# The last gate of a two-layer decoder trunk, with the operands of its matmuls exchanged

## The chip, the cores and the metric

The kernel runs on one core of one Trainium2 chip. The metric is the device time of one execution in microseconds (us). Engines: PE is TensorE, DVE is VectorE, ACT is ScalarE, POOL is GpSimd, SP issues most DMAs. Everything is float32; most matmuls run in the form fp32r, with each operand split into a high and a low part.

## The reference, cut to what matters

```python
D_MODEL, SEQ, PLE_DIM, DEPTH = 1024, 512, 256, 2
for i in range(DEPTH):
    h = h + mixer_i(rmsnorm(h, norm_mix[i]))          # two kinds of attention
    h = h + squared_relu_mlp(rmsnorm(h, norm_mlp[i]), w_ff1[i], w_ff2[i])
    gate = jax.nn.sigmoid(rmsnorm(h, norm_ple[i]) @ w_ple_gate[i])
    h = h + gate * (p[i] @ w_ple_proj[i])
return rmsnorm(h, final_norm)
```

The change is in the last pass through the two `gate` lines (i = 1) and in the final `rmsnorm`. `h` is 512 x 1024, `w_ple_gate[1]` is 1024 x 1024, `w_ple_proj[1]` 256 x 1024.

## The kernel before, in words

Activations lie with features on partitions: `h_b` is 8 slabs (KC) of 128 features x 512 tokens (T); a block of 128 tokens is one of NT = 4. Work is cut into units. A unit makes 128 output features for all tokens: its weights (128 rows x 8 row blocks x 128 columns, for the gate 8 + 2 with `w_ple_proj`) are loaded into `w_raw` by SP, split by ACT into `w_hi` and by DVE into `w_lo`, and multiplied on PE. Units alternate between two buffers and two PSUM banks (`unit_out`). For each row block `passes` issues three matmuls (hi x hi, hi x lo, lo x hi), with the weights stationary and 512 tokens moving:

```python
def passes(bank, w_k, hi, lo, start, stop):
    te.matmul(bank, w_k[0], hi, start=start, stop=False)
    te.matmul(bank, w_k[0], lo, start=False, stop=False)
    return te.matmul(bank, w_k[1], hi, start=False, stop=stop)
```

The order on every engine is written out by hand, and engines meet through semaphores. The gain of a norm is folded into the activations; the root of a norm multiplies the output of a unit (`scaled = unit_out * rstd`), so it is needed only when the first unit is evacuated. For that `statistics` sums the squares over partitions with a matmul against ones, ACT takes the root and DVE the reciprocal, all on 128 x 512.

The last gate (`gate_of(1, U_BG, 5, None)`) has units n = 0 to 6; the eighth is done in two halves of 256 tokens (`end_unit(0)`, `end_unit(1)`). For each unit DVE evacuates `unit_out` into `scaled`, ACT takes the sigmoid, DVE multiplies by the projection and adds the slab of `h_b`, ACT squares the slab (POOL adds up `sumsq`) and multiplies it with the final gain into `h_a`, PE turns that back to tokens on partitions (`turn_back`, four 128x128 transposes), and DVE copies it to `y_out` (`turned_back`). At the end, for each half: column sums of the squares with one-column matmuls (`end_sum`), root (`end_stat`), reciprocal, and each block of 128 tokens of `y_out` scaled by its root (`end_row`, two on DVE, two on ACT) and sent out by SP. ACT loads its table for the square root ahead, by a root of a spare column between the two halves.

An earlier stage already has tokens stationary (`values_unit`), with 512 weight columns moving.

Of the kernel before, what the change touches and what calls it, by code (L numbers as in the profile page):

```python
# [38 lines left out]
P = 128  # L39
# [203 lines left out]
def build(nc, x, p, rel_bias, a_w_qkv, a_w_o, b_w_qkv, b_w_o, lq1, lk1, lq2, lk2, subln, norm_mix,  # L243
          norm_mlp, w_ff1, w_ff2, norm_ple, w_gate, w_proj, final_norm, selector, out):
    ctx = ExitStack()
    with ctx:
# [64 lines left out]
        end_col = sb("end_col", [P, NT])  # L311
        end_scale = sb("end_scale", [P, NT])
# [24 lines left out]
        y_out = heads[:, KC * T:2 * KC * T].rearrange("p (a c) -> p a c", c=D)  # L337
        vectors = nc.dram_tensor("bias_vectors", (HEADS, VEC), F32, kind="Internal")
# [25 lines left out]
        def end_sums(hf):  # L364

            return (attn, unit_out[(U_END - 1) % 2])[hf][:, 0:NH]

# [8 lines left out]
        def end_turn_bank(hf):  # L376

            return wide_bank(2 + hf)[:, 0:HALF]

        def end_bank(n):  # L380

            return wide_bank(1 + n % 3)

# [215 lines left out]
        f_ready = sem("f_ready")  # L599
        ft_ps = sem("ft_ps")  # L600
        f_copied = sem("f_copied")
# [3 lines left out]
        end_ps = sem("end_ps")  # L605
# [55 lines left out]
        def _(sp):  # L661
# [141 lines left out]
            load_out(U_BO, 1, b_w_o[0])  # L803
            load_mlp(U_BF, 1)
# [8 lines left out]
        def _(pool):  # L813
# [44 lines left out]
            for norm in range(1, 7):  # L858
                for n in range(1, KC if norm < 6 else KC - 1):
                    pool.wait_ge(square_ready, (norm - 1) * (KC - 1) + n)  # L860
                    pool.wait_ge(sumsq_done, (norm - 1) * KC + n)
                    pool.tensor_tensor(sumsq[:, :], sumsq[:, :], square[n % 2][:, :],  # L862
                                       ALU.add).then_inc(sumsq_done, 1)


        @block.scalar
        def _(sc):
# [43 lines left out]
            def statistics(norm):  # L911
                sc.wait_ge(stat_ps, norm + 1)
                sc.activation(root[:, :], attn[:, :], ACT.Sqrt, scale=1.0 / D,
                              bias=eps_col[:, 0:1]).then_inc(root_ready, 1)
# [146 lines left out]
            def gate_of(layer, first, norm, dst):  # L1061
                for n in range(KC):
                    u = At(first + n)
                    if n == 0:
                        next_hi(u)
                        sc.wait_ge(sumsq_done, norm * KC)
                        sc.activation(sumsq_parts[:, 0, :], sumsq[:, :], ACT.Copy).then_inc(sumsq_hi_ready, 1)
# [8 lines left out]
                    slab((norm + 1) * KC + n, n, h_b, dst, gated_ready, layer * KC + n + 1)  # L1076
                    if layer == 0 and n == 1:
                        split_ple_hi(1)
                    if layer == 1:

                        col = gain_col((norm + 1) * KC + n)
                        sc.activation(h_a[:, n, :], h_b[:, n, :], ACT.Copy, scale=gains[:, col:col + 1]
                                      ).then_inc(f_ready, 1)
# [54 lines left out]
            last, w = KC - 1, 7 * KC - 1  # L1138
            gain = gains[:, gain_col(w):gain_col(w) + 1]
# [6 lines left out]
            def end_slab(hf):  # L1146
                cols = slice(hf * HALF, (hf + 1) * HALF)
                sc.wait_ge(gated_ready, 2 * KC + hf)
                sc.activation(square[w % 2][:, cols], h_b[:, last, cols], ACT.Square
                              ).then_inc(square_ready, 1)  # L1150
                sc.activation(h_a[:, last, cols], h_b[:, last, cols], ACT.Copy, scale=gain
                              ).then_inc(f_ready, 1)

            def end_stat(hf):
                sc.wait_ge(end_ps, hf + 1)
                sc.activation(end_col[:, hf * NH:(hf + 1) * NH], end_sums(hf), ACT.Sqrt, scale=1.0 / D,
                              bias=eps_col[:, 0:1]).then_inc(end_root, 1)

            def end_row(hf):
                a = hf * NH + 1  # L1160
                sc.wait_ge(f_copied, KC + hf)
                sc.wait_ge(end_rstd, hf + 1)
                sc.activation(y_out[:, a, :], y_out[:, a, :], ACT.Copy, scale=end_scale[:, a:a + 1]
                              ).then_inc(y_ready_odd, 1)

            end_sigmoid(0)
            sc.wait_ge(sumsq_done, w - 1 - KC)
            end_slab(0)
            end_sigmoid(1)

            sc.activation(spare[:, :], eps_col[:, 0:1], ACT.Sqrt)
            end_stat(0)
            end_slab(1)
            end_row(0)
            end_stat(1)
            end_row(1)
# [3 lines left out]
        def _(ve):  # L1180
# [24 lines left out]
            def statistics(norm):  # L1205
                ve.wait_ge(root_ready, norm + 1)
                ve.reciprocal(rstd[:, :], root[:, :]).then_inc(rstd_ready, 1)
# [249 lines left out]
            def turned_back(n):  # L1457

                ve.wait_ge(ft_ps, n + 1)
                ve.tensor_copy(y_out[:, :, n * P:(n + 1) * P],  # L1460
                               end_bank(n).rearrange("p (a c) -> p a c", c=P)).then_inc(f_copied, 1)

            def gate_of(layer, first, norm, dst):

                for n in range(KC):
                    u = At(first + n)
                    if n == 0:
                        next_lo(u)
                        ve.wait_ge(sumsq_hi_ready, layer + 1)
# [7 lines left out]
                    ve.tensor_tensor(scaled[:, :], unit_out[u.const % 2][:, :], rstd[:, :], ALU.mult  # L1477
                                     ).then_inc(evac_done, 1)
# [11 lines left out]
                    else:  # L1490
                        ve.tensor_tensor(h_b[:, n, :], hidden[:, :], h_b[:, n, :], ALU.add
# [5 lines left out]
                    if layer == 1 and n > 1:  # L1497
                        turned_back(n - 2)
# [102 lines left out]
            def end_evac(hf):  # L1601
                cols = slice(hf * HALF, (hf + 1) * HALF)
                ve.wait_ge(units_done, U_END + hf)
                ve.tensor_tensor(scaled[:, cols], end_unit_bank(hf), rstd[:, cols], ALU.mult
                                 ).then_inc(evac_done, 1)

            def end_gated(hf):
# [3 lines left out]
                                 ).then_inc(ple_ps_done, 1)  # L1611
                ve.wait_ge(ple_ps_done, 2 * KC + hf)
                ve.tensor_tensor(h_b[:, last, cols], hidden[:, cols], h_b[:, last, cols], ALU.add
                                 ).then_inc(gated_ready, 1)

            def end_turned(hf):
                ve.wait_ge(ft_ps, KC + hf)
                ve.tensor_copy(y_out[:, hf * NH:(hf + 1) * NH, last * P:(last + 1) * P],
                               end_turn_bank(hf).rearrange("p (a c) -> p a c", c=P)
                               ).then_inc(f_copied, 1)  # L1620

            def end_row(hf):
                a = hf * NH
                ve.wait_ge(end_root, hf + 1)
                ve.reciprocal(end_scale[:, a:a + NH], end_col[:, a:a + NH]).then_inc(end_rstd, 1)
                ve.wait_ge(f_copied, KC + hf)
                ve.wait_ge(end_rstd, hf + 1)
                ve.tensor_scalar(y_out[:, a, :], y_out[:, a, :], end_scale[:, a:a + 1], None, ALU.mult
                                 ).then_inc(y_ready_even, 1)

            turned_back(last - 2)
# [6 lines left out]
            end_row(0)  # L1638
            end_turned(1)
            end_row(1)  # L1640


        @block.tensor
        def _(te):
# [290 lines left out]
            def gate_of(layer, first, norm):  # L1935
                for n in range(KC):
                    u = At(first + n)
                    if layer == 1 and n == KC - 1:
                        break
# [17 lines left out]
                    if layer == 0 and n == 1:  # L1957
                        turn_ple(1)
                    if layer == 1 and n > 1:
                        turn_back(n - 2)  # L1960

            def turn_back(n):

                te.wait_ge(f_ready, n + 1)
                wait(te, f_copied, n - 2)
# [144 lines left out]
```

## Time and profile before

| | |
|---|---|
| median of 3 runs | 1614.56 us (1613.98 to 1615.56) |
| the profiled execution | 1614.48 us |
| its span, first to last instruction | 1612.6 us |
| PE busy | 1598.4 us |
| DVE, ACT, POOL busy | 906.3, 607.3, 65.9 us |
| mean granted clock of TensorE | 0.998 of full speed |

The span is the time between the first and the last instruction; the execution's own time is 1.9 us longer. Durations of matmuls overlap, as they are pipelined: the distance between the starts of two of them is what PE gives to one.

### The profile page before, as it was taken

The numbers are of one execution on the slowest core, as the hardware profiler recorded it, in microseconds if no ns is written. First come the engines' busy times: TensorE is split into PE (matmuls) and PEld (weight loads), VectorE is DVE, ScalarE is ACT, GpSimd is POOL, SyncE is SP. The second block draws the span as 40 slices with busy tenths as digits, with TensorE's granted clock in tenths as the row PEclk, the third lists the DMA queues.
The fourth block names the chain that finished last, engine by engine and source line by source line (L and its number), as shares of the span: only waits on it lengthen the run. The fifth ranks groups of instructions, "written<-read, shape, count | busy, mean of one in ns | idle before, by whom it ended". The sixth has DMA issues, their size and how long they took to land.

```text
span 1612.6 us, 22051 instructions
## 1 busy us (share of the span) xinstructions
PE 1598.4 (99%) x8244; PEld 1319.4 (82%) x8244; DVE 906.3 (56%) x1585; ACT 607.3 (38%) x1092; POOL 65.9 (4%) x68
## 2 busy tenths in 40 slices
PE   9999999999999999999999999999999999999998
PEld 7888888888888788888888878888878888888887
DVE  5365464464455863635455676777675363535555
ACT  5234334333333531312223445676652222222344
POOL 1000000000000200000001110000020000000111
PEclk9999999999999999999999999999999999999999
DMA  6633433433322333333333333323233333333331
GB/s 165 161 105 96 127 104 93 120 112 86 101 84 69 105 91 103 93 96 94 97 92 103 98 111 92 92 80 93 62 92 103 93 91 104 91 104 91 92 111 72
DMA packets 300571, 160.12 MB, mean 99 GB/s; under 512 B 31545, under 2 KB 295282, under 8 KB 300514
## 3 DMA queue, kind: packets, MB, share of 16 engines
q1 hardware_dynamic: 300112, 158.61, 34.6%
q0 software_dynamic: 144, 0.71, 0.2%
q8 instruction: 37, 0.61, 0.2%
q14 instruction: 20, 0.16, 0.0%
q10 hardware_dynamic: 258, 0.04, 0.0%
HBM read 157.11 MB, written 10.60 MB: 104 GB/s over the span
## 4 chain that ended last, share of the span: by engine, by line
PE 95%; POOL 1%; DVE 1%; DMA 1%; ACT 1%; issue 0%; SPq 0%; POOLq 0%; ACTq 0%; DVEq 0%
PE unit_out L1647 26%; PE unit_out L1649 26%; PE unit_out L1648 25%; PE turned L1723 2%; PE attn L1792 2%; POOL sumsq L862 1%; PE attn L2037 1%; PE unit_out L1811 1%; PE logits L1723 1%; PE unit_out L1812 1%; PE unit_out L1813 1%; DMA w_raw<-in_a_w_qkv_dram 1%; PE logits L1647 1%; PE misc L1723 1%; PE misc L1647 1%; PE misc L1649 1%
## 5 line engine op out<-in xcount | busy, mean ns | idle before, releaser
L1647 PE MATMUL unit_out<-act_hi,w_hi 128*128 128x512 f32 x1849 | 726.5, 393 | 1.4 <-DVE act_lo L1202 1.0
L1649 PE MATMUL unit_out<-act_hi,w_lo 128*128 128x512 f32 x1849 | 718.7, 389 | 0.0
L1648 PE MATMUL unit_out<-act_lo,w_hi 128*128 128x512 f32 x1849 | 718.0, 388 | 0.0
L880 ACT ACTIVATE w_hi<-w_raw 128x1024 fp32r<-128x1024 f32 (+3 forms) x256 | 271.0, 1058 | 459.4 <-PE unit_out L1649 348.2
L1647 PEld LDWEIGHTS unit_out<-act_hi,w_hi 128*128 128x128 f32 x1849 | 347.2, 188 | 76.3 <-DVE w_lo L1187 2.8
L1649 PEld LDWEIGHTS unit_out<-act_hi,w_lo 128*128 128x128 f32 x1849 | 347.1, 188 | 72.5
L1648 PEld LDWEIGHTS unit_out<-act_lo,w_hi 128*128 128x128 f32 x1849 | 347.5, 188 | 69.7 <-issue 0.2
L1187 DVE TENSOR_TENSOR w_lo<-w_raw,w_hi 128x1024 fp32r<-128x1024 f32 (+3 forms) x256 | 320.2, 1251 | 119.3 <-ACT w_hi L880 119.3
L1049 ACT ACTIVATE act_hi<-hidden 128x512 fp32r<-128x512 f32 x64 | 40.5, 633 | 243.4 <-DVE hidden L1445 243.4
L862 POOL TENSOR_TENSOR sumsq<-sumsq,square 128x512 f32<-128x512 f32 x41 | 57.8, 1410 | 1523.9 <-ACT square L908 1522.2
L1442 DVE TENSOR_TENSOR scaled<-unit_out,rstd 128x512 f32<-128x512 f32 x62 | 42.8, 690 | 67.8 <-PE unit_out L1649 67.7
L1266 DVE TENSOR_TENSOR h_a<-h_a,unit_out 128x512 f32<-128x512 f32 x39 | 26.8, 687 | 90.0 <-PE unit_out L1649 90.0
L1266 DVE TENSOR_TENSOR heads<-heads,unit_out 128x512 f32<-128x512 f32 x40 | 27.5, 686 | 84.2 <-PE unit_out L1649 84.2
L988 ACT ACTIVATE probs<-probs,w_raw 128x256 f32<-128x256 f32 (+1 forms) x128 | 61.7, 483 | 32.4 <-DVE w_raw L1290 32.4
L1448 DVE TENSOR_TENSOR act_lo<-hidden,act_hi 128x512 fp32r<-128x512 f32 x64 | 44.3, 692 | 44.7 <-ACT act_hi L1049 44.7
L1445 DVE SCALAR_TENSOR_TENSOR hidden<-scaled 128x512 f32<-128x512 f32 x64 | 44.3, 692 | 2.2
L1526 DVE CUSTOM_DVE_ANT_0 probs<-logits,bias 128x512 f32<-128x512 f32 (+3 forms) x64 | 28.2, 486 | 26.0 <-PE logits L1649 26.0
L1105 ACT ACTIVATE probs<-probs,low 128x512 f32<-128x512 f32 (+3 forms) x64 | 35.4, 554 | 7.4 <-DVE low L1526 7.4
L895 ACT ACTIVATE act_hi<-heads,gains 128x512 fp32r<-128x512 f32 x24 | 17.3, 722 | 49.1 <-DVE heads L1266 25.6
L1358 DVE TENSOR_TENSOR act_lo<-attn,act_hi 128x512 f32 (+1 forms) x8 | 5.5, 690 | 53.6 <-ACT act_hi L1002 53.6
L1275 DVE TENSOR_SCALAR probs<-probs,w_raw 128x256 f32<-128x256 f32 (+1 forms) x128 | 35.2, 339 | 0.3
L1290 DVE CUSTOM_DVE_ANT_0 probs<-logits,bias 128x256 f32<-128x256 f32 (+1 forms) x64 | 21.1, 386 | 20.4 <-PE logits L1774 20.4
(291 smaller groups left out, 1414.4 us busy)
## 6 DMA issues: line engine op xcount, KB each, us to landing
w_raw<-in_w_ff_dram SPq DMA_DIRECT2D x128, 512.0 KB, 4.0
w_raw<-in_a_w_qkv_dram SPq DMA_DIRECT2D x56, 512.0 KB, 3.9
w_raw<-in_b_w_qkv_dram SPq DMA_DIRECT2D x24, 512.0 KB, 5.1
w_raw<-in_a_w_qkv_dram SPq DMA_DIRECT2D x32, 256.0 KB, 3.0
w_raw<-in_w_ple_gate_dram SPq DMA_DIRECT2D x16, 512.0 KB, 4.1
bias_tiles_b<-bias_vectors SPq DMA_DIRECT2D x16, 256.0 KB, 4.3
bias<-bias_tiles_b SPq DMA_DIRECT2D x8, 512.0 KB, 3.7
w_raw<-in_a_w_o_dram SPq DMA_DIRECT2D x8, 448.0 KB, 3.6
```

The source lines that it names most:

```text
L862: pool.tensor_tensor(sumsq[:, :], sumsq[:, :], square[n % 2][:, :], ALU.add).then_inc(sumsq_done, 1)
L880: sc.activation(weights_of(u)[0][:, 0:width, :], w_raw[par][:, 0:width, :], ACT.Copy).then_inc(hi_done, 1)
L988: e = sc.activation(probs[i][:, cols], probs[i][:, cols], ACT.Exp, bias=low_col, scale=-1.0, accum_out=sum_col)
L1187: ve.tensor_tensor(lo[:, 0:width, :], w_raw[par][:, 0:width, :], hi[:, 0:width, :], ALU.subtract).then_inc(lo_done, 1)
L1266: ve.tensor_tensor(h[:, n, :], h[:, n, :], unit_out[u.const % 2][:, :], ALU.add).then_inc(evac_done, 1)
L1442: ve.tensor_tensor(scaled[:, :], bank_of(u)[:, :], rstd[:, :], ALU.mult).then_inc(evac_done, 1)
L1445: ve.scalar_tensor_tensor(hidden[:, :], scaled[:, :], 0.0, scaled[:, :], ALU.max, ALU.mult).then_inc(hid_ready, 1)
L1448: ve.tensor_tensor(MID[layer][1][:, n, :], hidden[:, :], MID[layer][0][:, n, :], ALU.subtract).then_inc(hid_done, 1)
L1647: te.matmul(bank, w_k[0], hi, start=start, stop=False)
L1648: te.matmul(bank, w_k[0], lo, start=False, stop=False)
L1649: return te.matmul(bank, w_k[1], hi, start=False, stop=stop)
L1723: last = te.transpose(bank[:, dst:dst + P], src, ident[:, :])
```

## The change: what it does

- In the last gate the operands of the matmuls are exchanged: a block of 128 tokens is stationary, the 128 weight columns of the unit move (`token_passes`, for each of 4 token blocks). The output has tokens on partitions and goes into the same bank, 4 blocks of 128 x 128.
- The root of the norm ahead of it has one value for each partition and block: the sum of squares comes from four one-column matmuls (`token_statistics`), root and reciprocal are on 128 x 4 instead of 128 x 512. The split of `sumsq` into high and low parts is dropped for this layer.
- The residual `h_b` is turned (`turn_h(n)`, behind unit n) instead of the sum; the eighth slab is turned ahead of the two halves.
- The final sum of squares runs along the free axis: ACT squares four blocks of 128 x 128 for each slab with an accumulator into `end_squares`, and for each half DVE adds the 8 numbers of each token (`reduce_sum`).
- The final gain, now along the free axis, is loaded as 128 copies of 1024 numbers into `end_gain` (512 KB, on SP's queue between the output projection's loads and the last MLP's), and POOL multiplies slabs 0 to 6 with it, DVE the last.
- At the end ACT has the order sigmoid 0, squares 0, sigmoid 1, root 0, squares 1, root 1, without the root of the spare column; DVE scales rows 0 to 2, ACT row 3.

```diff
@@ sync
             load_out(U_BO, 1, b_w_o[0])
+            sp.wait_ge(logits_done, ITEMS_A + B_HEADS * B_ITEMS)
+            sp.dma_start(end_gain, final_norm.rearrange("(n c) -> n c", n=1)[0:1, :].partition_broadcast(P)
+                         ).then_inc(end_gain_ready, 16)
             load_mlp(U_BF, 1)
@@ gpsimd
+            pool.wait_ge(end_gain_ready, 16)
+            for n in range(KC - 1):
+                pool.wait_ge(end_squared, n + 1)
+                pool.tensor_tensor(slab_of_y(n), slab_of_y(n), gain_of_slab(n, NT), ALU.mult
+                                   ).then_inc(y_gained, 1)
@@ scalar, gate_of
+                        sc.wait_ge(gated_ready, KC + n + 1)
+                        wait(sc, end_squared, n - 1)
+                        for a in range(NT):
+                            done = sc.activation(square[n % 2][:, a * P:(a + 1) * P],
+                                                 y_out[:, a, n * P:(n + 1) * P], ACT.Square,
+                                                 accum_out=end_squares[:, a, n:n + 1])
+                        done.then_inc(end_squared, 1)
-                        sc.activation(h_a[:, n, :], h_b[:, n, :], ACT.Copy, scale=gains[:, col:col + 1]
-                                      ).then_inc(f_ready, 1)
@@ vector, gate_of
-                        ve.tensor_tensor(h_b[:, n, :], hidden[:, :], h_b[:, n, :], ALU.add
+                        ve.wait_ge(h_turned_ps, n + 1)
+                        ve.tensor_tensor(slab_of_y(n), by_token(hidden[:, :]), by_token(end_bank(n)), ALU.add
                                          ).then_inc(gated_ready, 1)
-                    if layer == 1 and n > 1:
-                        turned_back(n - 2)
@@ vector, end
             end_evac(0)
             end_gated(0)
+            end_sum(0)
             end_evac(1)
-            turned_back(last - 1)
             end_gated(1)
-            end_turned(0)
-            end_row(0)
-            end_turned(1)
-            end_row(1)
+            end_scales(0)
+            end_row(0, y_ready_even)
+            end_row(1, y_ready_odd)
+            end_sum(1)
+            end_scales(1)
+            end_row(2, y_ready_even)
@@ tensor
+            def token_passes(bank, blocks, w_k, src, k, start, stop):
+                for n, a in enumerate(blocks):
+                    to = bank[:, n * P:(n + 1) * P]
+                    hi, lo = (x[:, k, a * P:(a + 1) * P] for x in src)
+                    te.matmul(to, hi, w_k[0], start=start and n == 0, stop=False)
+                    te.matmul(to, hi, w_k[1], start=False, stop=False)
+                    last = te.matmul(to, lo, w_k[0], start=False, stop=stop and n == len(blocks) - 1)
+                return last
+            def token_gate(first, norm):
+                ple = ple_hi[1], ple_lo[1]
+                for n in range(KC - 1):
+                    u = At(first + n)
+                    te.wait_ge(lo_done, u.const + 1)
+                    te.wait_ge(evac_done, u.const - 1)
+                    for k in range(KC):
+                        if n == 0:
+                            te.wait_ge(act_ready, norm * KC + k + 1)
+                        if n == 1 and k == 3:
+                            token_statistics(norm)
+                        token_passes(unit_out[u.const % 2], range(NT), weights(u.const % 2, k), IN[1], k,
+                                     k == 0, k == KC - 1)
...
+                    turn_h(n)
@@ tensor, end
-            turn_back(last - 2)
+            turn_h(KC - 1)
             end_unit(0)
             end_unit(1)
-            turn_back(last - 1)
-            end_sum(0)
-            end_turn(0)
-            end_sum(1)
-            end_turn(1)
```

## Rows read from the trace of the kernel before

**Rows 1.** The page: busy time by engine, and the chain by engine.
```profile
PE 1598.4 (99%) x8244; PEld 1319.4 (82%) x8244; DVE 906.3 (56%) x1585; ACT 607.3 (38%) x1092; POOL 65.9 (4%) x68
...
PE 95%; POOL 1%; DVE 1%; DMA 1%; ACT 1%; issue 0%; SPq 0%; POOLq 0%; ACTq 0%; DVEq 0%
```

**Rows 2.** Busy time in the last gate: length, each engine (instructions), clock, DMA.
```profile
1543.00:1602.00 59.00, 58.77 (x300) 49.70 (x299) 34.67 (x42) 26.25 (x36) 9.11 (x7) 1.00 0.23 67
```

**Rows 3.** Timeline of DVE (start, length): the evacuations at the gate's ends.
```profile
1543.45 0.69 DVE L1266 TENSOR_TENSOR heads<-heads,unit_out 128x512 f32<-128x512 f32 x1 [0.70 <-PE unit_out L1649]
...
1601.98 0.42 DVE L1604 TENSOR_TENSOR scaled<-unit_out,rstd 128x256 f32<-128x256 f32 x1 [1.81 <-PE misc L1649]
```

**Rows 4.** Timeline of PE and its weight loads (PEld): 512 columns, then 256.
```profile
1592.13 0.19 PEld L1647 LDWEIGHTS misc<-ple_hi,w_hi 128*128 128x128 f32 x1
...
1593.27 0.19 PEld L1649 LDWEIGHTS misc<-ple_hi,w_lo 128*128 128x128 f32 x1
...
1594.51 0.36 PE L1647 MATMUL unit_out<-act_hi,w_hi 128*128 128x256 f32 x1
...
1601.66 0.28 PE L1649 MATMUL misc<-ple_hi,w_lo 128*128 128x256 f32 x1
```

**Rows 5.** Timeline: transposes, then two fp32r loads; groups: one transpose's mean.
```profile
1593.72 1.03 PE L1723 MATMUL turned<-ident,h_a 128*128 128x128 f32 x8
...
1594.48 0.19 PEld L1647 LDWEIGHTS unit_out<-act_hi,w_hi 128*128 128x128 f32 x1
...
1594.59 0.19 PEld L1648 LDWEIGHTS unit_out<-act_lo,w_hi 128*128 128x128 f32 x1
...
L1723 PE MATMUL turned<-ident,h_a 128*128 128x128 f32 x20 | 3.1, 275 | 0.0
```

**Rows 6.** Other 128-column matmuls: timeline, then the chain, then a load group.
```profile
1059.74 0.19 PEld L1648 LDWEIGHTS logits<-qk_lo_b,qk_hi 64*128 64x128 f32 x2
...
1059.85 0.20 PEld L1649 LDWEIGHTS logits<-qk_hi,qk_lo_b 64*128 64x128 f32 x2
...
1058.31 1.05 PE L2037 MATMUL attn<-heads,probs_t 128*128 128x128 f32 x8
...
1059.29 0.39 PE L1647 MATMUL logits<-qk_hi 64*128 64x256 f32 x2
...
534.21 3.43 PE attn L1792 x60
...
L1792 PEld LDWEIGHTS attn<-probs,heads 128*64 128x64 f32 x480 | 26.0, 137 | 2.8 <-issue 2.8
```

**Rows 7.** The chain: a one-column fp32 matmul, two records.
```profile
1605.33 0.22 PE unit_out L2074 x2
```

**Rows 8.** Groups of weight loads where tokens are stationary: the second of a pair.
```profile
L1812 PEld LDWEIGHTS unit_out<-w_lo,act_hi 128*128 128x128 f32 x64 | 12.0, 188 | 2.2
```

**Rows 9.** One tile: ACT's squares with an accumulator (min/median/max ns).
```profile
L1119 ACT ACTIVATE square<-square x4: 294/295/312, 1168.0 to 1168.9; 128x128 f32<-128x128 f32 x4
```

**Rows 10.** Timeline of the tail, ACT and DVE.
```profile
1602.88 1.28 ACT L1171 ACT_TABLE_LOAD   x1
...
1604.83 0.75 DVE L1628 TENSOR_SCALAR heads<-heads,end_scale 128x1024 f32<-128x1024 f32 x1
...
1606.90 1.15 ACT L1163 ACTIVATE heads<-heads,end_scale 128x1024 f32<-128x1024 f32 x1 [0.49 <-DVE end_scale L1625]
```

**Rows 11.** SP's timeline, the chain, and the page's DMA issues (KB, us).
```profile
1174.17 0.34 SPq L675 DMA_DIRECT2D w_raw<-in_b_w_o_dram  x1
...
1178.13 3.99 DMA w_raw<-in_w_ff_dram
...
bias<-bias_tiles_b SPq DMA_DIRECT2D x8, 512.0 KB, 3.7
```

**Rows 12.** Timeline of PE at the start: transposes of the identity.
```profile
1.74 3.67 PE L1729 MATMUL unit_out<-ident 128*128 128x128 f32 x16 [1.74 <-POOL ident L819]
...
8.28 1.97 PE L1729 MATMUL unit_out<-ident 128*128 128x128 f32 x16
```

More of the change, by code:

```diff
@@ L912, in statistics @@
                 sc.wait_ge(stat_ps, norm + 1)
-                sc.activation(root[:, :], attn[:, :], ACT.Sqrt, scale=1.0 / D,
+                to, sums = (start_col[:, :], attn[:, 0:NT]) if norm == 5 else (root[:, :], attn[:, :])
+                sc.activation(to, sums, ACT.Sqrt, scale=1.0 / D,
                               bias=eps_col[:, 0:1]).then_inc(root_ready, 1)
@@ L1137, in _ @@
             gate_of(1, U_BG, 5, None)
-            last, w = KC - 1, 7 * KC - 1
-            gain = gains[:, gain_col(w):gain_col(w) + 1]
+            last = KC - 1
             def end_sigmoid(hf):
@@ L1956, in gate_of @@
                     last.then_inc(units_done, 1)
-                    if layer == 0 and n == 1:
+                    if n == 1:
                         turn_ple(1)
[L1959 to L1965, printed above, removed]
-                turn(end_bank(n), [(a * P, h_a[:, n, a * P:(a + 1) * P])
-                                   for a in range(NT)]).then_inc(ft_ps, 1)
+            def token_passes(bank, blocks, w_k, src, k, start, stop):
[6 more added lines that the diff above has]
+                return last
@@ new lines, in token_statistics @@
+            def token_statistics(norm):
+                te.wait_ge(sumsq_done, norm * KC)
+                for a in range(NT):
+                    last = te.matmul(attn[:, a:a + 1], sumsq[:, a * P:(a + 1) * P], ones[:, 0:1],
+                                     start=True, stop=True)
+                last.then_inc(stat_ps, 1)
+            def token_gate(first, norm):
[5 more added lines that the diff above has]
+                    for k in range(KC):
+                        if n == 0:
+                            te.wait_ge(act_ready, norm * KC + k + 1)
[3 more added lines that the diff above has]
+                                     k == 0, k == KC - 1)
+                    if n == 0:
+                        te.wait_ge(ple_ready, 2)
+                    te.wait_ge(ple_ps_done, KC + n - 1)
+                    for k in range(KP):
+                        last = token_passes(ple_bank(n), range(NT), weights(u.const % 2, KC + k), ple, k,
+                                            k == 0, k == KP - 1)
+                    last.then_inc(units_done, 1)
+                    turn_h(n)
@@ L1969, in _, with turn_h @@
+            def turn_h(n):
+                wait(te, gated_ready, KC + n - 2)
+                turn(end_bank(n), [(a * P, h_b[:, n, a * P:(a + 1) * P]) for a in range(NT)]
+                     ).then_inc(h_turned_ps, 1)
             out_late(0, U_AO)
@@ L2044, in _ @@
             mlp_of(1, U_BF, 4)
-            gate_of(1, U_BG, 5)
-            last, u = KC - 1, U_END - 1
+            token_gate(U_BG, 5)
+            u = U_END - 1
             def end_unit(hf):
-                cols = slice(hf * HALF, (hf + 1) * HALF)
+                blocks = range(hf * NH, (hf + 1) * NH)
                 te.wait_ge(lo_done, u + 1)
```

145 lines of the change are left out of this document (71 added, 74 removed).

## The prediction

> **What bounds the kernel now.** I read the page first, then the last 70 us stage by stage. The page gives TensorE (PE) 1598.4 us of a 1612.6 us span, and PE holds 95% of the chain that ended last [rows 1]. So a change in PE's own work is paid in full, and work on the other engines is free until it makes PE wait. The stretch that the diff rewrites is the last gate. Over 59 us of it PE is busy for 58.77, VectorE (DVE) for 34.67, ScalarE (ACT) for 26.25 and GpSimd (POOL) for 9.11 [rows 2]. PE binds here too, and the others have 40% or more of their time to spare. I measure the stage between two evacuations by DVE that wait for PE: that of the last MLP unit at 1543.45 and that of the second half of the last gate unit at 1601.98, so 58.5 us [rows 3].
>
> The question is then what one matmul costs PE, which is the distance between starts, not the duration printed beside it. In a run of 128x512 matmuls the weight loads start at 1592.13 and, five later, at 1593.27: 0.228 us each. The 60 matmuls of 128x256 in the two half units start from 1594.51 to 1601.66: 59 steps of 0.121 us [rows 4]. The stage adds up: 7 units x 30 x 0.228 = 47.9, the two statistics matmuls 0.46, six slabs of four transposes 2.6, 60 x 0.121 = 7.3, in all 58.3 of 58.5.
>
> **Where the change puts its cost: the gate's matmuls.** Before, the stationary operand is a 128x128 block of weights and the moving one 512 tokens: three matmuls for each of 8+2 row blocks of the weights, 30 a unit. After, the stationary operand is a block of 128 tokens and the moving one the 128 weight columns. That is three matmuls for each of 4 token blocks: 12 for each row block, 120 a unit. Seven units give 840, and the two halves with 2 token blocks each 2 x 60 = 120, so 960 instead of 270. The columns streamed are the same, but each matmul brings its own weight load, and there are 3.6 times as many.
>
> So the price of a 128-column matmul with a 128-column load decides everything. No row has it with all 128 rows in fp32r; the nearest are these.
> - The eight transposes with 128 columns and 128x128 loads take 1.03 us, the last of them 0.275 in its own: (1.03 - 0.275) / 7 = 0.108 each. Right after them two fp32r loads with the full 128 rows start 0.11 apart (1594.48 and 1594.59) [rows 5].
> - The score matmuls of 128 columns in fp32r, on 64 rows, go as pairs in two halves of the array. Their loads start 0.11 apart from pair to pair (1059.74, 1059.85), so a half of the array takes a load each 0.11. Eight records of an fp32 128x128 product hold PE from 1058.31 to 1059.29: 0.1225 each, at most [rows 6].
> - A matmul that streams one column and still loads 128 takes two records in 0.22 us: 0.11 each, although there is nothing to stream [rows 7].
> The last row shows that it is the load that takes 0.11, and that 128 columns of streaming (a quarter of 0.228, 0.057) vanish beneath it. I take 0.110, between 0.107 (the two 128-column spacings, rounded down) and 0.1225. Sum: 960 x 0.110 = 105.6; bounds 102.7 and 117.6.
>
> The Trainium skill, "TensorE: Matmul & The Clock Gate", section "Back-to-back issue gap", puts a stream of load and matmul pairs at about 81 ns for 128 columns, and its section on the weight path's fast load says that full loads of types other than FP32 are read faster. By 81 ns the gate would be 77.8 instead of 105.6. The trace disagrees: its fp32r loads stand 110 ns apart, like those in fp32, so the rows decide.
>
> A load can't be saved for the two neighbours that share a stationary block (hi tokens against hi, then lo weights): the earlier stage with tokens stationary shows 64 loads for the second of such a pair, as many as matmuls [rows 8].
>
> **The other parts.** Turning: before, seven whole slabs and two halves, 32 transposes in all, of which 6 slabs were inside the 58.5. After, eight slabs of the residual, all 32 transposes, stand ahead of the halves: 32 x 0.109 = 3.5. Statistics: four one-column fp32 matmuls, 8 records x 0.11 = 0.9, for 0.46. The reciprocal on 128x4 instead of 128x512 frees DVE, but PE's idle in the whole stage is only 59 - 58.77 = 0.23 [rows 2], so it gives at most that. New stage: 105.6 + 3.5 + 0.9 = 110.0, against 58.5: **+51.5**.
>
> DVE, ACT and POOL: per unit the change drops a copy from PSUM on DVE and the gain pass on ACT, adds four 128x128 squares on ACT (0.295 each [rows 9], 1.2 in all) and gives POOL a 128x512 product in place of its sum. A unit lasts 120 x 0.110 + 0.44 = 13.6 us on PE, and before, at 7.3 us a unit, every one of them kept up. Costed at nothing; without that cover ACT's 1.2 us would be the dearest. The new waits are of that kind too: DVE waits for the turned residual, which PE turns right behind the same unit; ACT waits for sums of squares two units back; POOL waits once for the gain, with only its own products behind. Each has a unit of 13.6 us to be met in.
>
> The tail, from the evacuation at 1601.98. Before: evacuation and sigmoid until the table load begins at 1602.88, the load 1.28, and after sums, turn and copy the last row is scaled from 1606.90 to 1608.05: 6.07 us [rows 10]. After, counted from the evacuation: sigmoid to 0.88, table load to 2.18, root to 2.45, two squares to 3.1. DVE does product, sum and gain to 2.35, then the reciprocal and rows 0 and 1 (0.75 each) to 4.25, and only behind them the sum, root and reciprocal of half 1 (some 0.8 together), so that rows 2 and 3 start at 5.05 and the last ends at 6.2. The removed sums and turns on PE are made up by the two rows that are queued before the second sum. **+0.15**, between -0.5 and +1. What lies behind it (the output transfers) doesn't change.
>
> The gain's transfer: 512 KB on SP's queue behind the last output-projection load at 1174.17 and ahead of the MLP's first load, issued at 1178.13 and 3.99 us on the way, which is on the chain. It waits for all scores of the differential attention, and behind it on the queue stand all loads of the last MLP and gate; but the loads ahead of it already wait for units that come after those scores, so its wait is over when SP gets there. A transfer of that size takes 3.7 us: 1174.5 + 3.7 = 1178.2, over by the time the next one's packets move [rows 11]. I take 0; if it ran fully in front of the load, the whole time that the load is late would go into the end, at most 3.7.
>
> Total +51.5 + 0.15 = +51.7. The profiled execution took 1614.48 us (span 1612.6 and 1.9 around it), the median is 1614.56: the same. 1614.5 + 51.7 = **1666 us**. Its own range: 102.7 + 4.4 - 58.5 - 0.5 = +48.1 (1662.6) to 117.6 + 4.4 - 58.5 + 1 = +64.5 (1679).
>
> **Rivals.**
> - *Streaming sets the price, loads hide (no change or a little faster).* The 60 records of the value product with 128 columns take 3.43 us, 0.057 each [rows 6]: the stage would be 54.7 + 4.4 = 59.1, +0.6, and the kernel 1615. It turns to faster below (58.5 - 4.4) / 960 = 0.0564 a matmul. But those records load only 64 columns, in 137 ns instead of 188. Chance 2%.
> - *Loads in fp32r are faster than the spacing shows.* Price between 0.06 and 0.10; at 0.080 it is 76.8 + 4.4 - 58.5 = +22.7, 1637 us. For it: no row has a long run of full fp32r loads with little streaming. Against it: 0.11 in [rows 5] and [rows 6]. 4%. (The 81 ns of the Trainium skill, same page and section, would be a case of this one.)
> - *PE's clock falls to 1.2 GHz in the stage, since half the time nothing streams.* The first idle transposes take 3.67 us for 16 ((3.67 - 0.275) / 15 = 0.226 each), the same 16 later 1.97 us (0.113) [rows 12]. At 0.226: 960 x 0.226 = 217, +163, 1778 us; a third of the stage so, about 1703. Against it: these two rows hold nothing but transposes with a load each, and it was in such work that PE went from the slow spacing to the fast one. Load and stream one after another (0.11 + 0.053) would give +102, 1717; the transposes at 0.108 exclude it for fp32. Together 7%.
> - *Main case*: 87%.
>
> **Numbers.** 1660 to 1681 holds the main case with its bounds and a little for the gain's transfer; the rest, 13%, lies outside, most of it farther than a range could usefully reach. A measurement of this kernel tells about 0.2% (3 us). Slower: 87 + 4 + 7 = 98%, less 1 for what I haven't seen: 97%. Same 2%, faster 1%.
>
> **What would show it.** Right: about 690 more PE matmuls; a gate unit of 13.6 us between evacuations; PEld starts 0.11 apart in runs of the new matmuls; 110 us from the last MLP evacuation to that of the last half; a granted clock at 1.00 throughout; the MLP's first load no later after the last output-projection load than 4 us. Wrong: spacing of 0.06 or 0.08 (loads hide), or 0.16 and more (serial or slow clock), or PE waiting within a unit for DVE, ACT or POOL.

## The result, and the profile after

| | before | after |
|---|---|---|
| median, same chip | 1614.65 us (1613.98 to 1615.56, 4 runs) | 1744.03 us (1737.77 to 1750.16, 4 runs) |
| ratio, 95% interval | | 1.0801, 1.0748 to 1.0853 |
| the profiled execution, its span | 1614.48, 1612.6 | 1738.29, 1736.5 |
| mean granted clock | 0.998 | 0.956 |

The change costs +129.4 us where +51.7 was forecast. The four runs are two pairs, 1737.77 and 1738.29, and 1749.78 and 1750.16; what the 12 us between the pairs fit comes below. The profiled execution is one of the first pair.

The page of after, with the lines that answer to [rows 1] and, between them, the granted clock in 40 slices:

```profile
PE 1718.1 (99%) x8924; PEld 1448.7 (83%) x8924; DVE 899.7 (52%) x1580; ACT 605.6 (35%) x1135; POOL 66.9 (4%) x69
...
PEclk9999999999999999999999999999999999995556
...
PE 95%; POOL 1%; DMA 1%; DVE 1%; ACT 1%; issue 0%; SPq 0%; POOLq 0%; ACTq 0%; DVEq 0%
```

PE has 680 matmuls more (about 690 expected), and it is still the chain. What is new is the middle line: three slices at 5, half speed, and a last one at 6, where all slices read 9 before. Busy time doesn't tell this from work: PE is 99% busy in both kernels.

The windows of the last gate in after, cut where the spacing changes (length, each engine's busy time with its instructions, granted clock, DMA share, GB/s), where [rows 2] is one line with clock 1.00:

```profile
1543.90:1564.90 21.00, 21.00 (x190) 21.00 (x190) 5.51 (x7) 5.86 (x7) 1.33 (x1) 1.00 0.32 94
1564.90:1711.70 146.80, 146.80 (x693) 146.80 (x693) 19.56 (x24) 17.25 (x59) 7.62 (x6) 0.50 0.05 14
1711.70:1725.10 13.40, 13.39 (x120) 13.25 (x119) 2.90 (x7) 2.40 (x13) 1.27 (x1) 1.00 0.00 0
```

The reader is to see three stretches. First 190 matmuls in 21.0 us: 0.11 each, as forecast. Then 693 in 146.8: 0.212 each, at a granted clock of 0.50, which is 1.2 GHz. Then 120 in 13.4, again 0.112 at full clock, 2.4 GHz. In none of them is PE idle (its busy time is the length of the window to 0.01), and the other engines are busy for a seventh of the middle one at most. So nothing waits for data; the same matmuls last twice as long.

The timeline of PE in after at the two turning points (start, duration):

```profile
1561.34 0.28 PE L1996 MATMUL unit_out<-w_hi,act_lo 128*128 128x128 f32 x1
1561.45 1.00 PE L2003 MATMUL attn<-ones,sumsq 128*128 128x1 f32 x8
1562.31 0.31 PE L1994 MATMUL unit_out<-w_hi,act_hi 128*128 128x128 f32 x1
...
1564.69 0.27 PE L1994 MATMUL unit_out<-w_hi,act_hi 128*128 128x128 f32 x1
1564.80 0.29 PE L1995 MATMUL unit_out<-w_lo,act_hi 128*128 128x128 f32 x1
1564.91 0.40 PE L1996 MATMUL unit_out<-w_hi,act_lo 128*128 128x128 f32 x1
1565.11 0.41 PE L1994 MATMUL unit_out<-w_hi,act_hi 128*128 128x128 f32 x1
...
1709.74 1.07 PE L1754 MATMUL logits<-ident,heads 128*128 128x128 f32 x4
1710.61 1.06 PE L1754 MATMUL turned<-ident,heads 128*128 128x128 f32 x4
...
1711.75 0.27 PE L1996 MATMUL unit_out<-w_hi,act_lo 128*128 128x128 f32 x1
1711.86 0.28 PE L1994 MATMUL unit_out<-w_hi,act_hi 128*128 128x128 f32 x1
1711.97 0.27 PE L1995 MATMUL unit_out<-w_lo,act_hi 128*128 128x128 f32 x1
```

The starts go from 0.11 to 0.21 apart at 1564.91. The last work of another kind ahead of that is the four one-column fp32 matmuls of the new statistics (L2003, eight records, 1561.45 to 1562.31, 0.86 us), 2.6 us earlier. The starts go back to 0.11 right behind the eight transposes of the last two slabs (from the third gate matmul behind them on). The price of the slow stretch: 146.8 x (1 - 0.112 / 0.213) = 69.6 us. Had the clock come back only later, the last 13.4 us would have lasted about twice that, 12 to 13 us more: the distance between the two pairs of runs, whose mean clocks are 0.955 and 0.956 in one and 0.947 in the other. The recorded means agree. Low from 1564.9 to 1711.7 only, the profiled run's mean would be 1 - 0.5 x 146.8 / 1736.5 = 0.958 (0.956 measured); low from 1564.9 to the end of a span of 1748.0, it would be 1 - 0.5 x 183.1 / 1748.0 = 0.948 (0.947 measured). So in the slower pair the clock seems not to have come back at all; no trace shows it.

The timeline of DVE and ACT at the ends of the stage and in the tail, where [rows 3] and [rows 10] are before:

```profile
1543.87 0.69 DVE L1288 TENSOR_TENSOR heads<-heads,unit_out 128x512 f32<-128x512 f32 x1 [0.70 <-PE unit_out L1680]
...
1725.13 0.42 DVE L1626 TENSOR_TENSOR scaled<-unit_out,start_scale 128x256 f32<-128x256 f32 x1 [3.91 <-PE misc L1996]
1726.02 1.28 ACT L1183 ACT_TABLE_LOAD   x1
1727.94 1.42 DVE L1658 TENSOR_SCALAR heads<-heads,end_scale 128x1024 f32<-128x1024 f32 x2
1729.28 0.16 DVE L1646 TENSOR_REDUCE end_total<-end_squares 128x2 f32<-128x16 f32 x1
1730.08 1.15 ACT L1196 ACTIVATE heads<-heads,end_scale 128x1024 f32<-128x1024 f32 x1 [0.31 <-DVE end_scale L1651]
```

The stage is 1725.13 - 1543.87 = 181.3 us (58.5 before, 110.0 forecast). The tail from there to the end of the last scaled row is 1731.23 - 1725.13 = 6.10 us (6.07 before).

### The profile page after: what moved, and what is told of

The parts are those of the page before. It is cut to its first block, busy times and chain, and to the rows that moved or that the text cites. A ratio compares the mean times of both kernels' runs of the same rounds, so it can differ in the third digit from the quotient of the medians.

```text
span 1736.5 us, 23447 instructions
## 1 busy us (share of the span) xinstructions
PE 1718.1 (99%) x8924; PEld 1448.7 (83%) x8924; DVE 899.7 (52%) x1580; ACT 605.6 (35%) x1135; POOL 66.9 (4%) x69
## 4 chain that ended last, share of the span: by engine, by line
PE 95%; POOL 1%; DMA 1%; DVE 1%; ACT 1%; issue 0%; SPq 0%; POOLq 0%; ACTq 0%; DVEq 0%
PE unit_out L1678 23%; PE unit_out L1680 23%; PE unit_out L1679 23%; PE unit_out L1996 3%; PE unit_out L1995 3%; PE unit_out L1994 3%; PE turned L1754 2%; PE attn L1823 2%; POOL sumsq L878 1%; PE attn L2103 1%; PE logits L1754 1%; PE unit_out L1842 1%; PE unit_out L1843 1%; PE unit_out L1844 1%; DMA w_raw<-in_a_w_qkv_dram 1%; PE logits L1678 1%
## 5 line engine op out<-in xcount | busy, mean ns | idle before, releaser
L1678 PE MATMUL unit_out<-act_hi,w_hi 128*128 128x512 f32 x1777 | 699.7, 394 | 1.4 <-DVE act_lo L1223 1.0
L1680 PE MATMUL unit_out<-act_hi,w_lo 128*128 128x512 f32 x1777 | 692.4, 390 | 0.0
L1679 PE MATMUL unit_out<-act_lo,w_hi 128*128 128x512 f32 x1777 | 691.6, 389 | 0.0
L1679 PEld LDWEIGHTS unit_out<-act_lo,w_hi 128*128 128x128 f32 x1777 | 333.9, 188 | 67.0 <-issue 0.2
L1994 PE MATMUL unit_out<-w_hi,act_hi 128*128 128x128 f32 x256 | 94.8, 370 | 0.0
L1996 PE MATMUL unit_out<-w_hi,act_lo 128*128 128x128 f32 x256 | 94.6, 369 | 0.0
L1995 PE MATMUL unit_out<-w_lo,act_hi 128*128 128x128 f32 x256 | 94.5, 369 | 0.0
L1994 PEld LDWEIGHTS unit_out<-w_hi,act_hi 128*128 128x128 f32 x256 | 73.6, 287 | 0.0
L1995 PEld LDWEIGHTS unit_out<-w_lo,act_hi 128*128 128x128 f32 x256 | 73.5, 287 | 0.0
L1996 PEld LDWEIGHTS unit_out<-w_hi,act_lo 128*128 128x128 f32 x256 | 73.5, 287 | 0.0
L1011 ACT ACTIVATE probs<-probs,w_raw 128x256 f32<-128x256 f32 (+1 forms) x128 | 61.8, 484 | 32.4 <-DVE w_raw L1312 32.4
```

The source lines that it names most:

```text
L1011: e = sc.activation(probs[i][:, cols], probs[i][:, cols], ACT.Exp, bias=low_col, scale=-1.0, accum_out=sum_col)
L1994: te.matmul(to, hi, w_k[0], start=start and n == 0, stop=False)
L1995: te.matmul(to, hi, w_k[1], start=False, stop=False)
L1996: last = te.matmul(to, lo, w_k[0], start=False, stop=stop and n == len(blocks) - 1)
```

## The experiments

What had to be explained is why the clock was halved. Two causes were open: the *train* (matmuls that stream 128 columns behind a load that takes twice as long; then any slow price is in the change's core), or the *columns* (the 0.86 us of one-column matmuls in that train); the expectation of experiment 1 calls them A and B. Each kernel was timed beside the kernel before. All are the changed kernel but for the edit shown, one-column statistics included where it isn't said otherwise.

**1. Statistics that stream 128 columns.** The same sums, 128 times over (ScalarE reads one column of each block of 128):

```diff
-                    last = te.matmul(attn[:, a:a + 1], sumsq[:, a * P:(a + 1) * P], ones[:, 0:1],
+                    last = te.matmul(attn[:, a * P:(a + 1) * P], sumsq[:, a * P:(a + 1) * P], ones[:, :],
                                      start=True, stop=True)
```

> The changed kernel with one edit: the four matmuls of the statistics in the second unit stream 128 columns of ones instead of one. The profile of the changed kernel showed TensorE's granted clock falling to 0.50 some 3 us after these one-column matmuls. Theory A (the long run of matmuls with 128 columns moving and a full load each lets the clock fall, whatever stands between): the clock falls all the same, time 1735 to 1755 us. Rival B (the one-column matmuls trip the clock): the clock stays at 1.00, 960 x 0.112 us for the gate, 1668 us.

Measured: 1668.36 us (1668.08 to 1669.0), before 1615.16, ratio 1.0328 (1.0311 to 1.0345), clock 0.998. The window over the gate:

```profile
1543.00:1653.00 110.00, 110.00 (x986) 109.84 (x984) 28.34 (x37) 25.55 (x79) 10.27 (x8) 1.00 0.12 37
```

986 matmuls in 110 us at 1.00, none slow. The evacuations at the ends of the stage:

```profile
1544.02 0.69 DVE L1288 TENSOR_TENSOR heads<-heads,unit_out 128x512 f32<-128x512 f32 x1 [0.70 <-PE unit_out L1680]
...
1655.39 0.42 DVE L1626 TENSOR_TENSOR scaled<-unit_out,start_scale 128x256 f32<-128x256 f32 x1 [3.91 <-PE misc L1996]
```

That is 111.4 us for the 110.0 of the forecast. The train alone does not halve the clock, and my first theory, that it does, fell: the one-column matmuls in it do. They cost 1744.0 - 1668.4 = 76 us, and not the 0.9 that they last.

**2. The train with 256 columns.** Two row blocks of weights move as one operand and each block of tokens is loaded half as often; only every second row block of the activations is used, so this computes another product. The one-column statistics stay:

```diff
+            def wide_passes(bank, blocks, par, k0, src, k, start, stop):
+                w = [x[par][:, k0 + k:k0 + k + 2, :].rearrange("p k c -> p (k c)") for x in (w_hi, w_lo)]
...
-                    for k in range(KC):
+                    for k in range(0, KC, 2):
```

> The changed kernel with two row blocks of the weights taken as one moving operand of 256 columns: half as many matmuls and loads in the last gate, the same number of columns streamed, everything else of the change kept. It computes another product there (the second row block is multiplied with the tokens' features of the first, and blocks share a bank), so that only its time is read. Theory A: 480 matmuls at 0.121 us = 58 us, the clock stays at 1.00 to the tail, about 1620 us (58.1 + 4.4 against 58.5 before is +4, tail +0.2). Rival C (it isn't the matmuls: the turns of the residual, the squares and products by token, or the gain's transfer cost most of the 129 us): more than 1650 us.

Measured: 1618.55 us (1618.01 to 1620.53, 10 runs), ratio 1.0023 (1.0013 to 1.0032), clock 0.998. PE's timeline:

```profile
1575.08 0.28 PE L1996 MATMUL unit_out<-w_hi,act_hi 128*128 128x256 f32 x1
1575.20 0.28 PE L1997 MATMUL unit_out<-w_lo,act_hi 128*128 128x256 f32 x1
```

0.12 apart, as in [rows 4]. With 480 matmuls instead of 960, +3.4 us of the +129 is left, and the one-column matmuls do no harm.

**3. Fillers in the train.** One extra matmul of 512 columns behind every row block, 88 in all (the expectation counts 84):

```diff
+            def filler(bank, k):
+                te.matmul(bank[:, :], IN[1][0][:, k, 0:P], IN[1][0][:, k, :], start=True, stop=True)
...
+                            filler(wide_bank(0) if n == 1 else attn, k)
```

> The changed kernel with work added: behind the twelve matmuls of each row block one matmul of 512 columns whose result nobody reads, 84 in all (none in the last two row blocks of the second unit and none elsewhere). Theory A: the array streams enough for the clock to stay at 1.00; the gate costs 960 x 0.112 + 84 x 0.227 + 4.4 = 131 us, the kernel about 1687 us, some 55 us faster than without the added work. Rival D (the clock falls by the number of weight loads, or by the time since the stage began): the clock falls as in the changed kernel, and the time is above 1760 us.

Measured: 1688.9 us (1688.64 to 1689.21), ratio 1.0454 (1.0437 to 1.0472). The clock of the gate stays at 1.00. 88 x 0.227 = 20.0 us of added work on the 1668.4 of experiment 1 gives 1688.4: the fillers cost their own time and nothing else. The kernel does 20 us more work than after and is 55 us faster.

**4. Every second unit with 256 columns** (units 1, 3, 5 and both halves, with the product of experiment 2 in them; the statistics stand in unit 1):

```diff
+                    if n % 2:
+                        for k in range(0, KC, 2):
...
+                            wide_passes(unit_out[u.const % 2], range(NT), u.const % 2, 0, IN[1], k,
+                                        k == 0, k == KC - 2)
```

> The changed kernel with units 0, 2, 4 and 6 of the last gate as they are and units 1, 3, 5 and the two halves with 256 columns moving (another product in these, so only the time is read): stretches of 13.5 us with 128 columns and of 7.3 us with 256 in turn. Theory A with a fall that needs a stretch as long as the 21 us that passed in the changed kernel: the clock stays at 1.00, gate 4 x 13.4 + 4 x 7.3 + 4.4 = 87 us, 1643 us. If it falls within each narrow unit and comes back in each wide one: 1655 to 1700 us, and the granted clock shows several changes. If the fall is decided by the one-column statistics alone (rival B): one fall, after them.

Measured: 1643.31 us (1642.97 to 1644.2), ratio 1.0174 (1.0157 to 1.0191), clock 1.00 in the gate. The units of 128 columns between keep their full clock.

**5. Four fillers right behind the one-column matmuls**, nowhere else:

```diff
                             token_statistics(norm)
+                            for _ in range(4):
+                                filler(wide_bank(0), k)
```

> The changed kernel with the one-column statistics as they are and four matmuls of 512 columns right behind them, whose result nobody reads. Theory E (the one-column matmuls trip the clock only because the run around them has too little streaming to make up for them): the clock stays at 1.00; the time is that with the wide statistics, 1668.4, plus 4 x 0.227: 1669.3 us. Rival F (matmuls of one column trip it in this place whatever follows): the clock falls some 3 us behind them, 1735 to 1755 us.

Measured: 1669.82 us (1669.29 to 1670.04), before 1614.53, ratio 1.034 (1.0323 to 1.0358). The window in which after is already slow:

```profile
1565.00:1569.00 4.00, 4.00 (x38) 4.00 (x38) 1.37 (x2) 1.69 (x9) 0.69 (x1) 1.00 0.00 0
```

0.9 us of streaming behind the 0.9 us of one-column matmuls takes the whole loss away.

**6. The columns moved.** Experiment 1, with four one-column matmuls (their result unused) in unit 4 instead:

```diff
+                        if n == 4 and k == 3:
+                            for a in range(NT):
+                                te.matmul(attn[:, a:a + 1], sumsq[:, a * P:(a + 1) * P], ones[:, 0:1],
+                                          start=True, stop=True)
```

> The kernel with the wide statistics (1668.4 us, clock at 1.00) with four one-column matmuls added in the fifth unit, 57 to 60 us into the gate; their result isn't read. Theory E: the clock falls there, some 3 us later, and doubles what is left of the gate, some 50 us: 1705 to 1722 us, depending on whether it rises again at the eight transposes ahead of the two halves, as in one profile. Rival G (it was the place in the changed kernel, shortly behind the start of the narrow run, and not the one-column matmuls in a narrow run): the clock stays, 1669.3 us.

Measured: 1702.51 us (1701.26 to 1714.06), ratio 1.0566 (1.0528 to 1.0605); three runs at 1701.26 to 1703.13 and one 12 us above them. The columns and the transposes in PE's timeline:

```profile
1603.87 1.00 PE L2020 MATMUL attn<-ones,sumsq 128*128 128x1 f32 x8
...
1673.09 1.07 PE L1754 MATMUL logits<-ident,heads 128*128 128x128 f32 x4
1673.96 1.06 PE L1754 MATMUL turned<-ident,heads 128*128 128x128 f32 x4
```

And the windows around them:

```profile
1600.00:1604.00 4.00, 4.00 (x39) 4.00 (x37) 3.11 (x4) 1.64 (x3) 0.00 (x0) 1.00 0.02 6
1604.00:1608.00 4.00, 4.00 (x36) 4.00 (x35) 0.00 (x0) 1.16 (x8) 1.28 (x1) 0.91 0.54 158
1608.00:1612.00 4.00, 4.00 (x20) 4.00 (x20) 0.00 (x0) 0.00 (x0) 0.00 (x0) 0.50 0.00 0
...
1674.00:1678.00 4.00, 4.00 (x31) 4.00 (x30) 1.40 (x3) 1.91 (x9) 0.48 (x1) 0.80 0.00 0
```

The fall went with the columns, from 1564.9 to about 1607.6, and the rise came behind the same eight transposes. 68.3 us lay between: 68.3 x 0.474 = 32.4, and 1668.4 + 0.9 + 32.4 = 1701.7. This is the run that ties cause to place. The one slower run (span 1712.3, mean clock 0.969) fits a clock that stayed low to the end: 1 - 0.5 x 104.7 / 1712.3 = 0.969.

**7. A burst after the fall.** The changed kernel, with 24 matmuls of 512 columns ahead of the third unit:

```diff
+                    if n == 2:
+                        for _ in range(24):
+                            filler(attn, 0)
```

> The changed kernel with 24 matmuls of 512 columns at the head of the third unit, about 7 us behind the fall of the clock; nobody reads them. Theory E with a low clock that needs dense work to rise: the clock rises within the burst and stays up; 1668.4 + about 7 us lost between the fall and the burst + 24 x 0.227 to 0.43 = 1681 to 1686 us. Rival H (once down in this stage the clock stays down): 1750 to 1770 us.

Measured: 1683.98 us (1682.91 to 1685.2), ratio 1.043 (1.0413 to 1.0447). The burst in PE's timeline, and the gate's next matmul:

```profile
1579.81 7.83 PE L1991 MATMUL attn<-act_hi 128*128 128x512 f32 x24
1587.48 0.22 PE L1998 MATMUL unit_out<-w_hi,act_hi 128*128 128x128 f32 x1
```

Windows behind the fall, and then in and behind the burst:

```profile
1564.00:1568.00 4.00, 4.00 (x21) 4.00 (x20) 1.37 (x2) 2.06 (x10) 0.31 (x1) 0.50 0.00 1
...
1580.00:1584.00 4.00, 4.00 (x11) 3.13 (x11) 2.79 (x4) 1.64 (x5) 0.00 (x0) 0.50 0.07 20
1584.00:1588.00 4.00, 4.00 (x21) 3.33 (x20) 0.00 (x0) 0.83 (x6) 1.29 (x1) 0.96 0.48 144
```

The clock falls as in after, is back in the burst, and stays for the rest. So it is a state that holds once entered, not a property of this work: the train runs on at whichever of the two speeds it has. The burst takes 7.7 us (5.4 at full clock) and saves 60.

**8. Two of the four one-column matmuls**, the other two with 128 columns:

```diff
+                    end = a * P + (P if a < 2 else 1)
+                    last = te.matmul(attn[:, a * P:end], sumsq[:, a * P:(a + 1) * P], ones[:, 0:end - a * P],
```

> The changed kernel with two of the four statistics matmuls streaming 128 columns and two streaming one. If any one-column work in the narrow run suffices for the fall: as the changed kernel, 1735 to 1755 us. If it depends on how much of it stands together: the clock stays, 1668.4 us; executions of both kinds would mean that half is about as much as it takes.

Measured: 1667.83 us (1667.62 to 1668.44), ratio 1.033 (1.0312 to 1.0347), no fall. Two of the four one-column matmuls leave the clock at full speed in all four runs. So an fp32 matmul of one column does not by itself bring the fall; four in a row did in all runs of after and of experiments 6 and 7.

**9 and 10. 192 and 64 columns.** The gate's matmuls of experiment 1 with 192 or 64 columns moving instead of 128, each a sum of its own (so another product), loads and counts unchanged. If the load sets the price, both keep the spacing:

```diff
+                w = [x[par][:, :, :].rearrange("p k c -> p (k c)")[:, first:first + 192] for x in (w_hi, w_lo)]
...
+                    to = bank[:, at0:at0 + 192]
...
+                    te.matmul(to, hi, w[0], start=True, stop=True)
```

> The kernel with the wide statistics (1668.4 us) and the same 960 matmuls and loads in the last gate, but each streams 192 columns instead of 128 and starts its own sum; the product is another one, so only its time is read. Theory L (the weight load of 128 columns sets the 0.112 us, and streaming hides beneath it as long as it is shorter): no change, 1668 to 1671 us. Rival M (streaming adds to a fixed cost per matmul): 64 columns more at 0.227 / 512 us each are 0.028 x 960 = +27, 1695 us.

> The kernel with the wide statistics (1668.4 us) and the same 960 matmuls and loads, each with 64 columns instead of 128; another product, only the time is read. Theory L says no change in the spacing, 0.112 us. Theory E says more: a run that streams only a quarter of the time can't hold the clock, which falls within the first unit or two, so some 95 us more, 1750 to 1780 us. If the clock stays: 1668 us. Rival M: 1641 us at full clock.

Measured with 192: 1669.36 us (1668.25 to 1670.33), before 1615.03, ratio 1.0333 (1.0316 to 1.0351), clock 1.00. PE's timeline with ten steps from first to last of these rows, 0.112 each:

```profile
1574.87 0.27 PE L1999 MATMUL unit_out<-w_hi,act_hi 128*128 128x192 f32 x1
...
1575.99 0.27 PE L2000 MATMUL unit_out<-w_lo,act_hi 128*128 128x192 f32 x1
```

Half as many columns again are free: the load is the price, as the prediction had it. Measured with 64: 1765.02 us (1764.4 to 1766.06), ratio 1.0929 (1.0911 to 1.0947), mean clock 0.939. Windows from the gate's start, and near its end:

```profile
1543.00:1547.00 4.00, 4.00 (x38) 3.99 (x36) 2.07 (x3) 2.40 (x3) 1.32 (x1) 1.00 0.55 164
1547.00:1551.00 4.00, 4.00 (x23) 4.00 (x22) 0.92 (x1) 0.00 (x0) 0.00 (x0) 0.57 0.37 113
...
1740.00:1750.00 10.00, 10.00 (x49) 10.00 (x48) 1.23 (x4) 0.69 (x4) 0.00 (x0) 0.50 0.00 0
```

The spacing starts at 0.11 (38 matmuls in 4 us) and is 0.213 from about 1547.3 on. No one-column matmul is in this train (its statistics are those of experiment 1, and stand behind the fall), and the eight transposes don't bring the clock back. With 64 columns the train does by itself what with 128 it did only with the one-column matmuls in it.

**11. Twice as many transposes.** The changed kernel, with every slab of the residual turned twice into the same place, so that eight transposes stand behind every unit:

```diff
-                turn(end_bank(n), [(a * P, h_b[:, n, a * P:(a + 1) * P]) for a in range(NT)]
+                turn(end_bank(n), [(a * P, h_b[:, n, a * P:(a + 1) * P]) for a in range(NT)] * 2
```

> The changed kernel, one-column statistics as they are, with each slab of the residual turned twice: eight transposes together behind each unit instead of four. In two profiles the clock rose right behind the eight transposes ahead of the two halves, in none behind four. Theory T (eight transposes together are what lets the clock rise in this stage): it rises behind the second or third unit, and the time is 1668.4 + 3.5 for the added transposes + 8 to 25 us at the low clock: 1680 to 1700 us. Rival: the rise came from something else, so the time is that of the changed kernel plus 3.5 to 7: 1740 to 1757 us.

Measured: 1680.41 us (1671.65 to 1681.84), ratio 1.0386 (1.0356 to 1.0415), clock 0.991 in the profiled run of 1681.84. PE's timeline behind the second unit:

```profile
1580.30 1.93 PE L1754 MATMUL turned<-ident,heads 128*128 128x128 f32 x8
```

And the windows there:

```profile
1580.00:1584.00 4.00, 4.00 (x21) 4.00 (x21) 2.77 (x3) 1.79 (x2) 0.00 (x0) 0.51 0.00 0
1584.00:1588.00 4.00, 4.00 (x38) 4.00 (x38) 0.70 (x2) 1.28 (x8) 1.28 (x1) 1.00 0.55 164
```

The clock comes back behind the first eight transposes that follow the fall, though not at once (they end at 1581.9, the rise is at 1584.0), and stays: 20.5 us slow, 9.7 lost, and 32 transposes of 0.109 for 3.5: 1668.4 + 3.5 + 9.7 = 1681.6. The one run at 1671.65 (clock 0.997) is what 1668.4 + 3.5 gives with next to no slow stretch, so four one-column matmuls did not bring a lasting fall in every run. In after four transposes stand behind each unit, and over five units they did not raise it. That doubling the transposes brings it back is shown; that it is their number, and not the time or the work that they add, is not.

## Why the prediction was wrong

The direction was right and the size was not. By its own steps:

- **The gate's matmuls, 960 x 0.110, between 0.107 and 0.1225: right.** At full clock they stand 0.112 apart, 107.5 us in all. With the one-column matmuls out of the way the kernel takes 1668.4 us (experiment 1) against the forecast 1666, inside its range of 1660 to 1681. Experiments 9 and 2 confirm the reason: from 128 to 192 columns nothing is added, and at 256 the price is 0.12, so it is the load. "Streaming sets the price" and "loads in fp32r are faster" are excluded. The Trainium skill, "TensorE: Matmul & The Clock Gate", section "Back-to-back issue gap", has about 81 ns for such a pair; the trace disagrees with 112.
- **"Statistics: four one-column fp32 matmuls, 8 records x 0.11 = 0.9": this is the step that failed.** Its duration is right (0.86 us), its cost is not: with what it does to the clock it is 76 us in the median. It was priced as an instruction among others, by what it occupies.
- **The rival "PE's clock falls to 1.2 GHz in the stage" came true and had 7%, together with another.** It was dismissed with [rows 12], idle transposes that went from the slow spacing to the fast one. That row shows a spacing that halves during transposes. The profile grants full clock there all along (1.00 over the first 5.4 us of the kernel before), so it doesn't even tie that halving to the granted clock. Nor does it show that a clock stays up in a train of loads with half the time nothing streaming, and still less with one-column matmuls in it. The prices that the rival named bracket the result: 1703 with a third of the stage slow, 1778 with all. The slow part was 693 of some 1000 matmuls: at 0.212 - 0.112 = 0.100 us more for each, that is +69 on the 1668.4 of experiment 1, and the profiled run took 1738.3. The test named for it, "a granted clock at 1.00 throughout", is what failed.
- **Turning, 32 x 0.109 = 3.5, and PE's idle of 0.23: right**, as 1668.4 - 1615.2 = +53.2 is 1.5 us over the forecast +51.7. The stage of experiment 1 has 1.4 of that (111.4 for 110.0), by matmuls a little over the 0.110 of the sum.
- **DVE, ACT and POOL at nothing: right.** They are busy for 19.56, 17.25 and 7.62 of 146.8 us at the low clock, and for 28.34, 25.55 and 10.27 of 110 at the full one (experiment 1), and PE waits for none of them in either.
- **The tail, +0.15: right**, +0.03 measured.
- **The gain's transfer, 0: right.** SP's queue has it at 1175.03, and the chain has the MLP's first load at 1178.61 with 3.94 us (1178.13 and 3.99 before, [rows 11]), with the stage's start moved by the same 0.4 to 0.5 us (1543.87 for 1543.45).

What is left open: which property of a stretch decides. The fall stood 2.6 us behind the one-column matmuls in after, 2.7 in experiment 6, 1.4 in experiment 7 and 0.6 in experiment 11, and nothing here says what sets that time. The clock rose behind eight transposes in the traces of after, experiment 6 and experiment 11, and behind four it did not; in the slower pair of runs of after and one run of experiment 6 the eight seem to have come without it, and with 64 columns they did. Nothing here separates their number from what stands around them.

No kernel here beats the one before. Without the fall the change costs 53 us, because its loads do. The nearest is the shape of experiment 2 at +3.4 us; with the right product it would need the weights of two units side by side, which was not built.

## What to carry to other kernels

Price a matmul by the larger of its load and its stream, and before exchanging operands count the loads: here 270 of them became 960, and the columns streamed stayed the same. In a stage where loads bind, look at the granted clock as a risk of its own, and ask of each short matmul in it not only how long it lasts: 0.86 us of one-column matmuls cost 76 us, and streaming 128 columns instead of one costs nothing, as the load is paid anyway. If busy shares read 99% and a stage is twice as long as its sum, look at the clock's line and at the spacing of starts before looking for waits.

## What the runs showed of the hardware

- TensorE's clock fell to 0.50 with no idle time on PE at all: in after (busy 21.00 of the 21.00 us ahead of the fall and 146.80 of the 146.80 behind it), and with 64 columns about 3.5 us into the gate (4.00 busy of 4.00 in the windows ahead and behind). The Trainium skill, "TensorE: Matmul & The Clock Gate", section "HAM oscillation — how this bites in real kernels", ties such falls to gaps in which PE waits; the traces here have the fall without a gap.
- Both speeds persist in the same work: 128-column matmuls behind full loads ran at 1.00 for 110 us (experiment 1) and at 0.50 for 146.8 us (after).
- At 0.50 the spacing set by the load goes from 0.112 to 0.213 us, 1.9 times, so the load follows the same clock.
- A clock that had fallen came back within 24 matmuls of 512 columns (experiment 7), with no pause of PE.
- At full clock, streaming one column, 64, 128 or 192 behind a full load costs the same 0.11 us; 256 costs 0.12.
